# A state-space scan of 64 steps instead of 256: the state kept at every fourth token, with the matrices for four tokens built earlier in the kernel

## The reference

```
ab = exp((lam_re + i lam_im) * dt);  bb = (ab - 1) / lam * b
bu[t] = bb @ u[t]                     # 16 channels -> 64 states, each group
s[t] = ab * s[t-1] + bu[t]            # 256 steps
y[t] = Re(c @ s[t]) + d * u[t]
y = gelu(y);  y = y * sigmoid(y @ w_glu + b_glu)
```

## Time and profile before

| | us |
|---|---|
| median of 3 runs | 2663.84 (2661.84 to 2665.62) |
| the profiled execution, its own time | 2666.63 |
| its span, first to last instruction | 2664.9 |
| PE busy | 2511.5 (94%) |
| DVE busy | 1834.2 (69%) |
| ACT busy | 1159.2 (44%) |
| POOL busy | 440.0 (17%) |
| mean granted clock of PE | 0.966 |

### The profile page before, as it was taken

One profiled execution on the slowest core, in us unless ns is written; L12 is line 12 of the kernel. 1 busy time (PEld: TensorE's weight loads), 2 busy tenths in 40 slices (PEclk: granted clock), 3 DMA queues, 4 the chain that ended last, 5 costly groups with the idle time before them and its releaser, 6 DMA issues.

```text
span 2664.9 us, 49308 instructions
## 1 busy us (share of the span) xinstructions
PE 2511.5 (94%) x17752; PEld 2340.7 (88%) x17752; DVE 1834.2 (69%) x2562; ACT 1159.2 (44%) x1636; POOL 440.0 (17%) x471
## 2 busy tenths in 40 slices
PE   7999999989999998789989888699999999999999
PEld 7999999889999998788877777699988888888888
DVE  7876676877765667777789999665555555555555
ACT  5454455644444446444442223234444444444443
POOL 3300000122000002111146677210100000000000
PEclk9999999999999999899888889799999999999999
DMA  6655554766555545444444545465677767767664
GB/s 231 216 182 189 177 175 158 226 207 215 177 172 178 179 149 188 152 160 128 134 152 142 162 156 161 139 210 182 187 194 189 186 186 187 186 186 187 183 187 160
DMA packets 212114, 474.04 MB, mean 178 GB/s; under 512 B 20264, under 2 KB 117204, under 8 KB 211776
## 3 DMA queue, kind: packets, MB, share of 16 engines
q1 hardware_dynamic: 182912, 415.29, 50.8%
q0 software_dynamic: 10016, 28.49, 3.7%
q10 hardware_dynamic: 19104, 29.15, 3.3%
HBM read 449.74 MB, written 25.84 MB: 178 GB/s over the span
## 4 chain that ended last, share of the span: by engine, by line
PE 64%; DVE 19%; issue 9%; ACT 3%; DMA 3%; POOL 1%; DVEq 0%; ACTq 0%; POOLq 0%
PE z_ps L1841 11%; PE z_ps L1843 11%; PE z_ps L1842 11%; DVE w_lo L1173 6%; PE z_ps L2124 6%; PE z_ps L2125 6%; PE z_ps L2130 6%; DMA tab_d<-arena 3%; PE o_ps L1880 1%; ACT w_hi L656 1%; PE s_ps L1862 1%; PE o_ps L2159 1%; PE o_ps L2158 1%; PE o_ps L2157 1%; PE p_ps L2158 1%
## 5 line engine op out<-in xcount | busy, mean ns | idle before, releaser
L1173 DVE TENSOR_TENSOR w_lo<-w_raw,w_hi 128x1024 fp32r<-128x1024 f32 x520 | 672.6, 1320 | 305.1 <-ACT w_hi L656 293.2
L1841 PE MATMUL z_ps<-x_hi,w_hi 128*128 128x256 f32 x2816 | 831.5, 295 | 35.4 <-DVE w_lo L1166 15.6
L1842 PE MATMUL z_ps<-x_lo,w_hi 128*128 128x256 f32 x2816 | 811.7, 288 | 0.0
L1843 PE MATMUL z_ps<-x_hi,w_lo 128*128 128x256 f32 x2816 | 810.8, 288 | 0.0
L656 ACT ACTIVATE w_hi<-w_raw 128x1024 fp32r<-128x1024 f32 x520 | 533.6, 1051 | 310.4 <-PE z_ps L1843 298.2
L1841 PEld LDWEIGHTS z_ps<-x_hi,w_hi 128*128 128x128 f32 x2816 | 556.3, 198 | 63.1 <-issue 51.3
L1842 PEld LDWEIGHTS z_ps<-x_lo,w_hi 128*128 128x128 f32 x2816 | 556.6, 198 | 1.3
L1843 PEld LDWEIGHTS z_ps<-x_hi,w_lo 128*128 128x128 f32 x2816 | 555.5, 197 | 0.0
L1731 DVE TENSOR_TENSOR w_lo<-w_raw,w_hi 128x1024 fp32r<-128x1024 f32 x262 | 320.7, 1225 | 314.9 <-ACT w_hi L1021 314.9
L1021 ACT ACTIVATE w_hi<-w_raw 128x1024 fp32r<-128x1024 f32 x262 | 277.7, 1060 | 427.8 <-PE z_ps L2130 271.0
L2124 PE MATMUL z_ps<-w_hi,x_hi 128*128 128x512 f32 x704 | 275.1, 391 | 0.6 <-DVE res L1707 0.6
(11 more groups left out here) (347 smaller groups left out, 3969.6 us busy)
## 6 DMA issues: line engine op xcount, KB each, us to landing
w_raw<-in_w SPq DMA_DIRECT2D x704, 512.0 KB, 4.1
w_raw<-in_w SPq DMA_DIRECT2D x80, 384.0 KB, 4.9
w_raw<-in_w SPq DMA_DIRECT2D x80, 128.0 KB, 2.8
tab_d<-arena ACTq DMA_DIRECT2D x32, 256.0 KB, 4.4
res<-tab_d POOLq DMA_DIRECT2D x32, 256.0 KB, 2.9
sg_d<-arena ACTq DMA_DIRECT2D x32, 128.0 KB, 3.1
arena<-sg_d POOLq DMA_DIRECT2D x16, 256.0 KB, 3.7
arena<-in_dil_bias ACTq DMA_DIRECT2D x12, 256.0 KB, 2.8
```

What stands on the lines that cost most here:

```text
L1173: dve.tensor_tensor(w_lo[:, n % RING, :], w_raw[:, n % RING, :], w_hi[:, n % RING, :].bitcast(F32), ALU.subtract).then_inc(w_lo_ready, 1)
L1841: pe.matmul(z, wh, hi[:, kt, :], start=(first and i == 0), stop=False)
L1842: pe.matmul(z, wh, lo[:, kt, :], start=False, stop=False)
L1843: m = pe.matmul(z, wl, hi[:, kt, :], start=False, stop=(last and i == len(kts) - 1))
```

## The change

Four tokens are treated at once. The state is kept at tokens 0, 4, 8, ..., so that a scan has 64 steps. For each tile three kinds of matrices of 128 rows are built on the chip: E (two of 128x128, from four tokens' input to the state), K (128x128, from four tokens' input to four tokens' output, with the skip term d on its diagonal), and F (two of 128x128, from the state to four tokens' output). With a table of cosine and sine for 64 steps they are 128x768 numbers a tile (`TAB`), stored in `tab_d`.

They are built in layer 1's head periods, two tiles a period, and no longer in the output periods. POOL's `tile_powers` multiplies c and b by the powers of `ab` in five rounds (`times`): each has two `tensor_scalar` and two `tensor_tensor` instructions with a wait after either pair. Four of the five rounds wait for `bt_ready`. PE's `tile` stands behind `attn_scores` (first tile, ahead of job 1) and behind `attn_turn` (second tile, ahead of job 3). It waits for POOL's last round, transposes twice, multiplies twice, and turns the next tile's b twice (`turn_b`). ACT's `tile` copies E and the turned b from PSUM (and so gives `bt_ready`), and then makes the table with `Sin`, `Square` and `Copy`. It stands behind `load_bias` and behind `probs_copy`. DVE's `tile` makes the angles (five operations of 64 columns) and adds d to K (four operations of 32 rows). The neighbourhood biases of layer 1, on POOL's queue, are made before the tiles.

In the gate periods two tiles make a pair, 16 pairs in 32 jobs, placed by the list `FRONT`. PE has 4 matmuls of 64 columns in `inputs` and 6 in `outputs`. DVE does modulation, scan and demodulation. POOL only issues transfers: the matrices of a pair once the pair before last is done, `u` in an order of its own, and the gelu's result out and back (`turn_back`), to bring it to token order. The gate loops of ACT, DVE and PE are written out. The last pair is done at job 27 and the last gelu at job 31.

```diff
 SPC = ST // CT
+STEP = 4
+NC = T // STEP
+PAIRS = ST // 2
+FRONT = (0, 2, 4, 6, 8, 9, 11, 12, 14, 16, 17, 19, 20, 22, 24, 25)
+TAB = 6 * P
...
+            def tile_powers(st, e, last=False):
+
+                x, at = xt[e], XT_STEPS * st
+                f_r, f_i = ssm_c[:, 0, bass.ds(st, 1)], ssm_c[:, 1, bass.ds(st, 1)]
+                l_r, l_i = ssm_lam[:, 0, bass.ds(st, 1)], ssm_lam[:, 1, bass.ds(st, 1)]
+                pool.wait_ge(bc_landed, 32 * (st + 1))
+                reach(pool, ek_done, st - 1)
+                reach(pool, f_stored, 16 * st)
+
+                def times(dst, src, t, re, im, k, size):
+
+                    pool.tensor_scalar(t, src, im, None, ALU.mult).then_inc(xt_step, 1)
+                    pool.tensor_scalar(dst, src, re, None, ALU.mult).then_inc(xt_step, 1)
+                    pool.wait_ge(xt_step, at + k + 2)
+                    for r, op in ((0, ALU.subtract), (1, ALU.add)):
+                        m = pool.tensor_tensor(dst[:, r], dst[:, r], t[:, 1 - r], op)
+                    m.then_inc(xt_step, 1)
+                    pool.wait_ge(xt_step, at + k + 3)
+
+                times(x[:, :, 0, :], c_in, xt_t[:, :, 0, :], f_r, f_i, 0, 1)
+                pool.wait_ge(bt_done, st + 1)
+                if not last:
+                    load_tile_in(st + 1)
+                pool.wait_ge(bt_ready, st + 1)
+                for m in range(3):
+                    times(x[:, :, m + 1:8 - m:6 - 2 * m, :], x[:, :, m:9 - m:8 - 2 * m, :], xt_t, l_r, l_i, 3 + 3 * m, 2)
+                times(x[:, :, 4, :], x[:, :, 3, :], xt_t[:, :, 0, :], l_r, l_i, 12, 1)
+                pool.dma_start(tab_d[st][:, 4 * P:TAB].rearrange("p (r b c) -> p r b c", r=2, b=4),
+                               x[:, :, 1:5, :]).then_inc(f_stored, 16)
...
+            with pool.Fori(0, KT) as n:
+                sum_squares(0, n, False)
+            for st in range(ST):
+                tile_powers(st, st % 2, last=(st == ST - 1))
+            pool.wait_ge(sums_ready, 2)
...
+            def load_pair(n):
+
+                for e in range(2):
+                    pool.dma_start(tab_in[:, 2 * (n % 2) + e, :], tab_d[2 * n + e]).then_inc(tab_landed[n % 2], 16)
...
+            for n in range(2, PAIRS):
+                pool.wait_ge(c_done, n - 1)
+                load_pair(n)
+                if n % 2 and n // 2 + 1 < CT:
+                    load_u(n // 2 + 1)
+                if n % 2 == 0 and n >= 4:
+                    turn_back(n // 2 - 2)
...
+            def b_turned(st, e, first=False):
+
+                bt_ps = tile_bank(v_ps if first else z_ps[1] if e == 0 else z_ps[3])[2]
+                act.wait_ge(bt_done, st + 1)
+                reach(act, ek_done, st)
+                act.activation(xt[e][:, :, 8, :], bt_ps, ACT.Copy)
+                for r in range(2):
+                    m = act.activation(btn[:, r, :].rearrange("p (j c) -> p j c", j=STEP),
+                                       bt_ps[:, r, :].unsqueeze(1).to_broadcast([P, STEP, 32]), ACT.Copy,
+                                       scale=1.0 - 2.0 * r)
+                m.then_inc(bt_ready, 1)
...
+            def tile(st, e, last=False):
+
+                act.wait_ge(ek_done, st + 1)
+                if not last:
+                    act.wait_ge(bt_done, st + 2)
+                reach(act, tab_stored, 16 * st)
+                act.activation(tab_out[:, 0:2 * P], tile_bank(z_ps[3 - 2 * e])[0], ACT.Copy).then_inc(e_ready, 1)
+                if not last:
+                    b_turned(st + 1, 1 - e)
                 act.wait_ge(turns_ready, st + 1)
-                if again:
-                    act.wait_ge(tab_stored, 16 * st)
...
                 act.wait_ge(tab_step, 2 * st + 2)
-                act.activation(tab_out[:, 0, :], turn_k[:], ACT.Copy, scale=-2.0, bias=1.0).then_inc(tab_ready, 1)
+                act.activation(tab_out[:, 3 * P:3 * P + NC], turn_k, ACT.Copy, scale=-2.0, bias=1.0).then_inc(tab_ready, 1)
                 act.wait_ge(tab_ready, st + 1)
...
                 if mem is not None:
                     mem_blocks(mem)
+                if l == 1:
+                    tile(2 * h, 0)
                 split_hi(p, 4)
                 if prev:
                     probs_copy(g - 1)
                 if mem is not None and mem_next:
                     mem_load(mem + 1)
+                if l == 1:
+                    tile(2 * h + 1, 1, last)
 
...
+            def tile(st, e, last=False):
+
...
+                dve.tensor_scalar(turns, turns, 0.5, -0.5, ALU.min, ALU.max).then_inc(turns_ready, 1)
+                dve.wait_ge(e_ready, st + 1)
+                if not last:
+                    dve.wait_ge(bt_ready, st + 2)
+                reach(dve, tab_stored, 16 * st)
+                for j in range(STEP):
+                    r = slice(32 * j, 32 * j + 32)
+                    m = dve.scalar_tensor_tensor(out=tab_out[r, 2 * P + 32 * j:3 * P], in0=ident[r, 32 * j:P],
+                                                 scalar=d_col[r, bass.ds(st, 1)], in1=k_ps[r, 0:P - 32 * j],
+                                                 op0=ALU.mult, op1=ALU.add)
+                m.then_inc(m_ready, 1)
...
+                dve.wait_ge(bu_done, n + 1)
+                bu = bu_ps[n % 2][:, 0, :].rearrange("p (e r k) -> p e r k", e=2, r=2)
+                dve.tensor_tensor(m2, bu, cos, ALU.mult)
+                dve.tensor_tensor(w2, bu, sin, ALU.mult).then_inc(bu_used, 1)
+                dve.wait_ge(bu_used, n + 1)
+                dve.tensor_tensor(vv[:, :, 0, :], m2[:, :, 0, :], w2[:, :, 1, :], ALU.add)
+                dve.tensor_tensor(vv[:, :, 1, :], m2[:, :, 1, :], w2[:, :, 0, :], ALU.subtract).then_inc(v_step, 1)
+                dve.wait_ge(v_step, 3 * n + 1)
+                for e in range(2):
+                    mag4 = ssm_mag[:, 2 * n + e:2 * n + e + 1].to_broadcast([P, NC])
+                    for r in range(2):
+                        m = dve.tensor_tensor_scan(vv[:, e, r, :], mag4, vv[:, e, r, :], 0.0, ALU.mult, ALU.add)
+                m.then_inc(v_step, 1)
+                dve.wait_ge(v_step, 3 * n + 2)
+                dve.tensor_tensor(m2, vv, cos, ALU.mult)
+                dve.tensor_tensor(w2, vv, sin, ALU.mult).then_inc(v_step, 1)
+                dve.wait_ge(v_step, 3 * n + 3)
+                if n >= 2:
+                    dve.wait_ge(c_done, n - 1)
+                dve.tensor_tensor(out[:, :, 0, :], m2[:, :, 0, :], w2[:, :, 1, :], ALU.subtract)
+                dve.scalar_tensor_tensor(out=out[:, :, 1, :], in0=w2[:, :, 0, :], scalar=-1.0, in1=m2[:, :, 1, :],
+                                         op0=ALU.mult, op1=ALU.subtract).then_inc(s_ready, 1)
+                dve.wait_ge(s_ready, n + 1)
...
+            def tile(st, e, p, last=False):
+
+                pe.wait_ge(z_free, taken(p, -1 if e == 0 else 1))
+                pe.wait_ge(xt_step, 15 * st + 15)
+                reach(pe, e_ready, st)
+                reach(pe, m_ready, st)
+                if not last:
+                    pe.wait_ge(bc_landed, 32 * (st + 2))
+                x = xt[e]
+                z = z_ps[3 - 2 * e]
+                e_ps, k_ps, _ = tile_bank(z)
+                for r in range(2):
+                    pe.transpose(e_ps[:, r * P:(r + 1) * P], x[:, r, 5:9, :].rearrange("p b c -> p (b c)"), ident[:])
+                for r in range(2):
+                    m = pe.matmul(k_ps, btn[:, r, :], x[:, r, 0:4, :].rearrange("p b c -> p (b c)"),
+                                  start=(r == 0), stop=(r == 1))
+                m.then_inc(ek_done, 1)
+                if not last:
+                    turn_b(z)
+
+            def head_period(p, l, h, kind, norm=False, prev=True, first=False, last=False):
...
+                if l == 1:
+                    tile(2 * h, 0, p)
+                    reach(pe, m_ready, 2 * h)
...
+                if l == 1:
+                    tile(2 * h + 1, 1, p, last)
+                    pe.wait_ge(m_ready, 2 * h + 1)
...
                     pe.wait_ge(rel_copied, N_DH)
+                    pe.wait_ge(bc_landed, 32)
+                    turn_b(v_ps)
...
+            def outputs(n):
...
+                    y = y_ps[j % 2][:, 0, s * NC:(s + 1) * NC]
+                    pe.matmul(y, tab[:, 2 * P:3 * P], u_in[j % 2][:, s, :], start=True, stop=False)
+                    for r in range(2):
+                        m = pe.matmul(y, tab[:, (4 + r) * P:(5 + r) * P], states[:, n % 2, e, r, 0:NC], start=False,
+                                      stop=(r == 1))
                 m.then_inc(c_done, 1)
...
+                    for n in range(PAIRS):
+                        if FRONT[n] == 4 * j + c:
+                            inputs(n)
+                        if FRONT[n] + 2 == 4 * j + c:
+                            outputs(n)
```

More of the change, by code:

```diff
@@ L971, in _ @@
             act.activation(y_hi[:, N_DH - 1, :], ov, ACT.Copy).then_inc(yo_hi, 1)
-            with act.Fori(2, CT) as j:
+            for j in range(2, CT):
```

(17 more changed lines are left out.)

447 lines of the change are left out of this document (232 added, 215 removed).

## The result

| | before | after |
|---|---|---|
| median, us | 2664.73 (4 runs, 2661.84 to 2666.91) | 2717.20 (4 runs, 2714.44 to 2719.99) |
| ratio, 95% interval | | 1.0189 (1.0172 to 1.0205) |
| span of the profiled execution, us | 2664.9 | 2715.0 |

The forecast was 2638, faster. The time lies near the upper end of the range.

The account below looks back on a forecast made before the run. PE was taken to bound the head periods and DVE the gate periods. The terms, -22 - 9 - 76 - 23 + 104 = -26 against the profiled 2666.6, gave 2640.6, or 2638 against the runs' median; the 8-in-10 range was 2560 to 2720.

Parts of the forecast that it names:

- Output periods, -22: Layer 1's output periods: without table work the waits for `w_lo` and `x_lo` shrink and clock returns, -22 us.
- Gate periods, -76: Gate periods: PE's and DVE's work shrinks, to 29.1 us a period in the last six; together -76 us.
- the gate stage gains half: Rival, gate periods: matrix transfers or DVE's order cost 4.5 us a period; sum +10, 2674 us; chance 0.10.
- Tail, -23: Between the last gate job and `w_glu`: the last pair is done four jobs before the end, -23 us.
- Layer 1's head periods, +104: Where the matrices are built: PE waits for POOL ahead of the second tile, 6.5 us a period, sixteen times, +104.
- Their price ... 5.2 us: Head periods: POOL's 16 instructions in four rounds behind `bt_ready`, priced from other rows, take 5.2 us.
- DVE's share: Head periods: time DVE's two splits for job 3 add to POOL's rounds, taken as 1.4 us, between 0 and 2.4.
- lost to the clock: Head periods: PE work lost at half clock behind the wait for POOL, taken as 2.0 us a period.
- POOL is the bound: Rival, head periods: rounds of 9.2 us and 2.0 from DVE, period 37.9 us, sum +70, 2734 us; chance 0.28.
- the forecast's own alternative: Head periods: by the skill's exclusion rule DVE's two splits add 2.4 us instead of 1.4; sum -10 instead of -26.
- The other half of the loop: Head periods, second tile to next first: `bt_ready` about 5 us behind, POOL 6.6 more, PE asks at 14.2.
- Layer 0's end, -9: End of layer 0: the 7.1 us table wait becomes about 1.6, with 3.4 us of clock regained, -9 us.

Follow-up runs that it names:

- e5: Changed kernel with ACT's copy of E and b, and DVE's D operation, moved earlier for the first tile in layer 1's head periods: 2696.0 us.
- e8: Changed kernel with POOL multiplying by constants instead of the two `ssm_lam` columns in the four rounds (computation changed): 2691.7 us.
- e10: Changed kernel with e6's edits, rounds divided between POOL and DVE, `softmax_scale` first, c's first two tiles before layer 1's norm: 2678.1 us, 1.0047 of before.
- e11: e10 with POOL loading the next b earlier, and DVE's first-tile angles earlier and D operation behind `softmax_scale` and k's evacuation: 2610.8 us.
- e1: Changed kernel without POOL's four rounds behind `bt_ready` from the third tile on (computation left out): 2626.1 us.
- e2: Changed kernel with POOL's stores counted on two semaphores in turn, so POOL waits only for the store before the last: 2706.6 us.
- e6: Changed kernel with the early turn of e5 and the two store semaphores of e2 together: 2638.9 us.
- e3: Changed kernel without the first of POOL's two one-input operations in the rounds behind the first (computation left out): 2640.6 us.
- e9: e6 with DVE's `softmax_scale` ahead of `split_lo(p, 3)`, `gate_silu` and `y_lower` in layer 1, rounds still on POOL: 2642.2 us.
- e12: e11 with DVE's evacuation of `gate_z` ahead of `split_lo(p, 1)` in layer 1's head periods: 2614.7 us, 0.9808 of before in 5 runs.

## Why the prediction was wrong

*Output periods, -22:* right, -21.8 in the same stretch. No wait for `w_lo` stands there any more.

*Gate periods, -76:* right, -75.0, and mostly by its parts: the first two periods gave 10.7 us against 15, the other six 64.3 against 61. That it is within 1 us is luck: with the same gate code the profiles of the twelve other runs have 246.0 to 254.9 us for these periods, a gain of 66 to 75. Eight of the 64-column records take 0.88 us, 0.11 each, the value taken between 0.055 and 0.22. DVE's splits are at 1.22 and the scans at 0.27 (0.28 forecast), and the clock is 0.99:

```profile
L1282 DVE TENSOR_TENSOR w_lo<-w_raw,w_hi 128x1024 fp32r<-128x1024 f32 x49 | 59.1, 1222 | 28.0 <-ACT w_hi L720 27.4
L1707 DVE TENSOR_TENSOR_SCAN arena<-ssm_mag,arena 128x64 f32<-128x64 f32 x52 | 10.9, 272 | 0.5
```

```profile
1689.68 1.08 PE L2224 MATMUL s_ps<-arena,res 128*128 128x64 f32 x8 [1.83 <-issue]
1690.56 0.36 PE L1970 MATMUL z_ps<-x_hi,w_hi 128*128 128x256 f32 x1
```

The last six periods took 28.6 us in the mean (29.1 forecast). They are uneven, 24.6 to 34.1, which I had not seen coming. The rival *the gate stage gains half* fell: no wait for a transfer is left in PE's list there.

*Tail, -23:* right, -23.9.

*Layer 1's head periods, +104:* the failed term. The mechanism was the forecast's: `bt_ready` at 8.8 us (9.1), PE's place for the second tile 13.2 us behind its first (13.0), one wait each ahead of the second tile, for POOL. What was mis-sized is the step "Their price ... 5.2 us", and next to it DVE's share:

| | forecast | measured |
|---|---|---|
| four rounds by themselves | 5.2 | 7.3 |
| DVE's share | 1.4 | 2.4 |
| PE's wait | 2.7 | 5.6 |
| first tile to second | 15.7 | 18.8 |
| lost to the clock | 2.0 | about 2.1 |
| second tile to the next first, with the clock | 16.2 | 16.7 to 17.3 |
| period | 31.9 | 35.5 to 36.1, steady |

Of the 3.9 us that the steady period is too long, 3.1 are POOL's rounds. The clock was sized rightly: its price is counted only where PE works. The two-input operations were nearly as forecast (0.30 and 0.23 us against 0.33 and 0.26). The one-input ones cost 0.60 and 0.44 and not 0.28 and 0.20: I had taken them from an operation of another kind, the one 128-column row. Carried down to 128 columns, the two-input rows that were at hand give 0.46, and four rounds of 6.6 us. The bound from above (0.535 each, 9.2 us) was in the text, and 0.61 us an instruction with DVE's share is past the 0.49 from which *POOL is the bound* decides. That rival is what happened, in a milder form: it gave 37.9 us a period and 2734.

DVE's share of 2.4 is also what the forecast's own alternative had, from the Trainium skill's rule (SBUF — State Buffer, Who interferes with whom). I had discounted it to 1.4; but POOL hardly pauses in its rounds, so the splits inside them meet an operation. That the two numbers agree to 0.1 us is partly luck: the alternative had two whole splits, and here the end of one and a pair lie in the rounds, 2.9 us of which 2.4 are added.

The other half of the loop was said to have slack, with 6.6 us for POOL behind `bt_ready`. It has next to none: with the store's landing, the round on c and 8.8 to 11.2 us of rounds POOL ends 0.1 to 1.3 us ahead of PE's first tile in the steady periods, so where the wait ahead of the second tile shrinks, POOL is late for the first, as in e5 and e8.

*Layer 0's end, -9:* the second failed term. With one second tile it was -9 + 6.5 = -2.5, and +19.6 was measured. I had kept one wait of about 1.6 us there, and in the profile after two of 10.0 and 7.9 us stand there, in layer 1's first head period, with 23.9 us at half clock around them. The first tile's rounds begin only when layer 0 ends and run into four of DVE's splits in a row:

```profile
551.29 2.46 POOL L559 TENSOR_SCALAR arena<-arena,ssm_lam 128x128 f32<-128x128 f32 x1
553.75 2.37 POOL L560 TENSOR_SCALAR arena<-arena,ssm_lam 128x128 f32<-128x128 f32 x1
```

The second is for DVE's D operation, which stands behind the norm of layer 1 in DVE's order. I had costed the steady chain and charged the first period the same. e10 and e11, with c's rounds done earlier and their D operation at another place, have 71 and 65 us for these two periods instead of 79.8. PE's wait of 10.0 us for POOL's first rounds is gone there; one of 5.6 and 5.8 us for an evacuation on DVE stays, and in e10 one of 3.3 for the load of b.

Two steps beside the sum were incomplete as well. e1 shows that without POOL the period is 28.6 and not 27.2, because DVE's D operation is late next. And e2, e5 and e6 show the landing of POOL's own store as a second hold-up behind the first.

## What to carry to other kernels

- Where several short operations of POOL lie between two steps of PE, price them by rows of the same kind (with their operands), and add the whole of each DVE operation that runs in their span. A factor of two in an instruction of 0.3 us was 2.1 of the 3.9 us by which each period was mis-sized.
- Divide such work by what it depends on, and order each engine by what PE asks for first: with c's rounds ahead of time on POOL, b's on DVE and `softmax_scale` early, the loss of 1.9% became a gain of 1.9%. No single edit did it, and several only moved the wait to what stood behind it.
- The first period of a stage needs its own chain, from what its inputs wait for.

## What the runs showed of the hardware

- POOL gets hardly anything done while DVE's operation on `w_lo` runs: with two SBUF inputs 2.9 us of it in the rounds added 2.4 (9.7 = 7.3 + 2.4), and with one, at 0.70 us for 1024 columns, 1.4 added 1.4 (8.7 = 7.3 + 1.4).
- A wait's price in clock: with waits of 5.6 us went 6.8 us at 0.50, of which PE worked through 4.8 in the mean and lost about 2.1. Behind waits of 1.8 us (e3) it was 3.4 us, all of it work. In the steady periods of e9 (1.55 us) and of e1 and e12 (about 1 us) the clock stayed at 1.00.
- POOL's one-input operation of 64 and 128 columns takes 0.44 and 0.60 us with a per-partition factor and 0.37 and 0.53 with a constant, longer than its two-input ones of half as many columns (0.23 and 0.30). Why the fixed part is larger with one input was not tried.
